# Output projection of a gated-delta-net block: feature halves of the first output units between the last chunk's steps

## The chip, the cores and the metric

The kernel runs on one core of one Trainium2 chip. The metric is the device time of one execution in microseconds; the kernel before took 1717.13 us in the median of three runs (1716.76 to 1719.14).

## What is computed

One block of a hybrid network over 16 meta tokens and 1024 tokens of 1024 features, all in fp32. A gated delta rule over chunks makes `o`; it is normalised per head, gated with `silu(z)`, and mixed with a causal pooling branch `y_b`. The mixed `y` goes through `w_out`, is added to the stream, and a convolved, gated MLP follows.

```python
def step(state, inp):
    q_i, k_i, u_i, w_i, qk_i, gt_i = inp
    v_new = u_i - jnp.einsum('bhck,bhkv->bhcv', w_i, state)
    o_i = jnp.einsum('bhck,bhkv->bhcv', q_i, state) + jnp.einsum('bhcs,bhsv->bhcv', qk_i, v_new)
    state = state * gt_i[..., None, None] + jnp.einsum('bhck,bhcv->bhkv', k_i, v_new)
    return state, o_i
...
o = (o * lax.rsqrt(jnp.mean(o * o, axis=-1, keepdims=True) + NORM_EPS)
     * head_norm.astype(jnp.float32) * jax.nn.silu(zf))
...
g_a, g_b = jnp.split(jax.nn.sigmoid(gate_pre), 2, axis=-1)
y = g_a * y_a + g_b * y_b
return jnp.einsum('bld,de->ble', y, w_out)
```

## The kernel before, in words

Every engine has one program written out by hand; the engines meet in counting semaphores only, and each queue works in the order in which the code stands. Features lie on the partitions, in eight tiles of 128 (`KT`), tokens along the free dimension.

**Products in three passes.** A large product takes an fp32 matrix apart into a high part (`u_hi`, `w_hi`) and what is left (`u_lo`, `w_lo`) and sums three matmuls for each of the eight feature tiles. A *unit* is one tile of 128 output features over one of three blocks of 342 tokens (`OBLOCKS`): 24 matmuls of 342 columns into one of three PSUM banks `gb`. Its weights are one tile of 512 KB: SyncE loads it to `w_raw`, ScalarE makes `w_hi` (`w_high`), GpSimd makes `w_lo` (`w_low`), three slots in turn. The semaphore `s_wlo` tells TensorE that a tile is ready.

**The chunks.** The delta rule runs over nine chunks of 128 tokens, all eight heads at once. A chunk has the steps P1 (keys times state), V (new values), O (outputs), SU (state) and OT (transposes of the output), besides those that invert a triangular matrix (X0 to Y2). In a chunk, matmul units of other projections stand between the steps to cover their latency; the last chunk's P1, V and O (L1153) have no units between them. After O, ScalarE copies the output from PSUM to `orx` and VectorE scales it with `output_scale`; `orx` is the buffer `vb`. `ot_d`, `za_d` and `yg_d` are DRAM tensors with each head's output, gated `z` and gated pooling branch. The last head's gates are still in `zs` and `gs`; `gated(8)` finishes `gs`, and ScalarE stores it to `yg_d`.

**The input of the output projection.** For each of the three token blocks `b`, SyncE's `load_y` brings `yo` from `ot_d`, `yz` from `za_d` and `yg` from `yg_d` (1.4 MB each) into one of two sets of buffers, block 2 into that of block 0. The second set lies where the chunk's buffers lay: `yo` of block 1 overlaps `vb`, so its load waits for OT. VectorE's `y_low` computes yo x yz + yg for the eight feature tiles in two halves of four; after each half ScalarE's `y_high` makes `u_hi` and VectorE subtracts to make `u_lo`, and counts `s_y`. `OUT_PLAN` gives the order of TensorE's work: units (0,0) and (1,0) (output tile, block), OT, then (2,0), (3,0), (4,0), (5,0), then (3,1), (4,1), (5,1), (3,2) and so on. Weight tiles 0 to 5 are used first, and tile `k` goes to the slot of `k - 3`. Tile 5 is loaded by SyncE behind block 1's `yz` and `yg` (L684), and ScalarE takes its high part after it evicts unit (2,0). Only the first unit of a block waits for `s_y`, once for each half.

## Time and profile before

| What | Time or count |
|---|---|
| Median of three runs | 1717.13 us (1716.76 to 1719.14) |
| Profiled execution, device time | 1718.44 us |
| Its span | 1716.6 us |
| TensorE, matmuls busy | 1675.1 us, 98% |
| VectorE busy | 896.9 us, 52% |
| ScalarE busy | 600.3 us, 35% |
| GpSimd busy | 494.5 us, 29% |
| Granted TensorE clock, mean | 0.994 of full speed |

Times in the timelines are microseconds from the start of the span. Busy time of a matmul is modelled and overlaps its neighbour, so TensorE's idle time before an instruction tells more than its busy share. The steps that the change touches lie between 830 and 890 us. PE is TensorE, DVE VectorE, ACT ScalarE, POOL GpSimd and SP SyncE; a q behind the name means the queue that issues DMAs.

### The profile page before, as it was taken

Reading aid. Unit: us, or ns where it says so; the run is one execution under the profiler, and the core shown is the slowest. Engines: PE = TensorE matmul, PEld = TensorE weight load, DVE = VectorE, ACT = ScalarE, POOL = GpSimd, SP = SyncE. Lnnn points to the kernel's source line nnn. Section 1 sums busy time; section 2 is a strip of 40 time slices with the busy share of each in tenths; the row PEclk is TensorE's granted clock in tenths of the full one; section 3 lists DMA queues with packets and bytes.
Section 4 is the critical chain, followed back from the end, with each engine's and each line's share of the span. In section 5 each row is a group of like instructions: output and inputs, shape, how many; then the busy total and the mean of one; then the engine's idle time right before and its main releaser. Section 6 shows DMA issues by size and latency. Waiting matters only on the chain.

```text
span 1716.6 us, 30495 instructions
## 1 busy us (share of the span) xinstructions
PE 1675.1 (98%) x12103; PEld 1603.8 (93%) x12103; DVE 896.9 (52%) x969; ACT 600.3 (35%) x982; POOL 494.5 (29%) x473
## 2 busy tenths in 40 slices
PE   7999999998999999999899999999999999999997
PEld 6999999998899999999899998998998998989986
DVE  5556454574444545444542665544545446455447
ACT  6333465544443434434333431221221211212214
POOL 3212212255445344453221132121212211221210
PEclk9999999999999999999999999999999999999999
DMA  5222443358555464554883121111111111211112
GB/s 182 71 93 97 131 147 90 92 157 142 149 167 140 119 158 114 141 163 109 208 270 97 38 62 50 37 49 49 49 37 39 59 49 37 61 48 38 49 37 98
DMA packets 242511, 168.23 MB, mean 98 GB/s; under 512 B 43913, under 2 KB 228840, under 8 KB 241306
## 3 DMA queue, kind: packets, MB, share of 16 engines
q1 hardware_dynamic: 209494, 135.30, 28.4%
q10 hardware_dynamic: 32740, 32.08, 5.6%
q8 instruction: 36, 0.59, 0.1%
q14 instruction: 17, 0.14, 0.0%
q0 software_dynamic: 224, 0.12, 0.0%
HBM read 125.10 MB, written 42.37 MB: 98 GB/s over the span
## 4 chain that ended last, share of the span: by engine, by line
PE 90%; DVE 3%; issue 2%; POOL 1%; POOLq 1%; ACT 1%; DMA 1%; DVEq 0%; ACTq 0%; SPq 0%
PE gb L878 66%; PE db L1224 11%; PE db L1022 4%; PE mb L1224 2%; PE db L936 1%; POOL w_lo L761 1%; PE db L1093 1%; PE db L1092 1%; DVE cacc L1735 1%; POOLq L810 1%; DMA yo<-ot_d 1%; POOLq L807 1%; DVE fino L2153 0%; PE db L1019 0%; PE db L1164 0%
## 5 line engine op out<-in xcount | busy, mean ns | idle before, releaser
L878 PE MATMUL gb<-u_hi,w_hi 128*128 128x342 f32 (+2 forms) x2520 | 821.9, 326 | 8.6 <-DVE u_lo L2021 5.1
L878 PE MATMUL gb<-u_lo,w_hi 128*128 128x342 f32 (+2 forms) x2520 | 809.5, 321 | 0.0
L878 PE MATMUL gb<-u_hi,w_lo 128*128 128x342 f32 (+2 forms) x2520 | 806.8, 320 | 0.0
L761 POOL TENSOR_TENSOR w_lo<-w_raw,w_hi 128x1024 fp32r<-128x1024 f32 x130 | 327.9, 2526 | 1048.8 <-ACT w_hi L1268 1048.7
L878 PEld LDWEIGHTS gb<-u_hi,w_hi 128*128 128x128 f32 x2520 | 477.4, 189 | 12.9 <-issue 9.2
L878 PEld LDWEIGHTS gb<-u_lo,w_hi 128*128 128x128 f32 x2520 | 477.6, 190 | 0.4
L878 PEld LDWEIGHTS gb<-u_hi,w_lo 128*128 128x128 f32 x2520 | 477.1, 189 | 0.0
L1268 ACT ACTIVATE w_hi<-w_raw 128x1024 fp32r<-128x1024 f32 x130 | 135.6, 1052 | 5.5 <-ACT tm L1367 5.2
L1735 DVE SCALAR_TENSOR_TENSOR cacc<-xb,prm,cacc 128x1040 f32<-128x1040 f32 x72 | 124.6, 1731 | 10.4 <-issue 8.4
L2118 DVE TENSOR_TENSOR h<-h,db 128x512 f32<-128x512 f32 x138 | 92.5, 684 | 42.2 <-PE db L1224 41.8
L1634 ACT ACTIVATE a_hi<-cv 128x1024 fp32r<-128x1024 f32 x21 | 22.3, 1060 | 248.8 <-PE db L1224 200.5
L1224 PE MATMUL db<-w_hi,a_hi 128*128 128x512 f32 x276 | 109.1, 395 | 0.1
L1224 PE MATMUL db<-w_lo,a_hi 128*128 128x512 f32 x276 | 109.1, 395 | 0.0
L1224 PE MATMUL db<-w_hi,a_lo 128*128 128x512 f32 x276 | 109.0, 395 | 0.0
L1619 ACT ACTIVATE xv<-gb 128x342 f32<-128x342 f32 x63 | 28.8, 458 | 188.1 <-PE gb L878 188.1
L2072 DVE TENSOR_SCALAR cg<-xg,prm 128x1024 f32<-128x1024 f32 x22 | 16.6, 754 | 138.9 <-ACT xg L1619 134.3
L1732 DVE TENSOR_SCALAR cacc<-xb,prm 128x1040 f32<-128x1040 f32 x24 | 18.3, 762 | 120.8 <-ACT xb L1389 96.6
L1389 ACT ACTIVATE xb<-gb 128x346 f32<-128x346 f32 (+1 forms) x63 | 28.8, 459 | 128.1 <-PE gb L878 128.0
L2074 DVE SCALAR_TENSOR_TENSOR cg<-xg,prm,cg 128x1024 f32<-128x1024 f32 x22 | 70.2, 3191 | 3.5 <-issue 3.4
L805 POOL TENSOR_TENSOR upd<-blk,sol 64x15 f32<-64x15 f32 (+4 forms) x135 | 48.4, 358 | 72.7 <-DMA blk<-blk_d 55.0
L1224 PEld LDWEIGHTS db<-w_hi,a_lo 128*128 128x128 f32 x276 | 51.7, 187 | 12.7
L1224 PEld LDWEIGHTS db<-w_hi,a_hi 128*128 128x128 f32 x276 | 51.8, 188 | 12.6 <-DVE a_lo L2142 0.5
(264 smaller groups left out, 1824.0 us busy)
## 6 DMA issues: line engine op xcount, KB each, us to landing
w_raw<-in_w_in SPq DMA_DIRECT2D x53, 512.0 KB, 4.2
w_raw<-in_w_up SPq DMA_DIRECT2D x44, 512.0 KB, 3.8
w_raw<-in_w_down SPq DMA_DIRECT2D x22, 512.0 KB, 3.5
qkT_d<-sl ACTq DMA_DIRECT2D x16, 576.0 KB, 2.8
kv_d<-tm ACTq DMA_DIRECT2D x16, 576.0 KB, 3.4
tk<-kv_d SPq DMA_DIRECT2D x9, 1024.0 KB, 7.6
w_raw<-in_w_out SPq DMA_DIRECT2D x11, 512.0 KB, 8.6
kT<-qkT_d SPq DMA_DIRECT2D x9, 512.0 KB, 5.0
```

The source lines that it names most:

```text
L761: pool.tensor_tensor(lo, w_raw[:, n % SLOTS, :], hi.bitcast(F32), ALU.subtract).then_inc(s_wlo, 1)
L805: pool.tensor_tensor(out, low[:, j, j + 1:].unsqueeze(2).broadcast_to([n, rest, j + 1]), inv[:, j, 0:j + 1].unsqueeze(1).broadcast_to([n, ...
L878: mm = pe.matmul(gb[:, bank, 0:w], wt, u, start=(k == 0 and m == 0), stop=(k == KT - 1 and m == 2))
L1022: return lambda o, m: pe.matmul(o, a[:, m, :], b[:, m, :], start=True, stop=True)
L1224: mm = pe.matmul(down_bank(u, n == W_LAST), a, wt, start=(q == 0 and m == 0), stop=(q == 1 and m == 2))
L1268: act.activation(wp_hi[:, :] if n == W_WPOOL else w_hi[:, n % SLOTS, :], w_raw[:, n % SLOTS, :], ACT.Copy).then_inc(s_whi, 1)
L1389: act.activation(xb[:, j % 3, 3 + o:3 + o + w], gb[:, b, 0:w], ACT.Copy).then_inc(s_gfree, 1)
L1619: act.activation(dst[:, o:o + w], gb[:, b, 0:w], ACT.Copy).then_inc(s_gfree, 1)
L1634: act.activation(a_hi[:, q, :], cv[:, :], ACT.Copy).then_inc(s_ahi, 1)
L1735: t = dve.scalar_tensor_tensor(cacc[:, :], xb[:, slot, j:j + T], tap(j), cacc[:, :], ALU.mult, ALU.add)
L2074: dve.scalar_tensor_tensor(dst[:, c0:c1], src[:, c0 + 1:c1 + 1], tap(1), dst[:, c0:c1], ALU.mult, ALU.add)
L2118: dve.tensor_tensor(dst, dst, down_bank(u, isinstance(i, int) and i == FFN_ITERS - 1), ALU.add).then_inc(s_dnfree, 1)
```

## The change

- **TensorE** runs the first feature halves of units (0,0), (1,0) and (2,0) early, the first between V and O, the others behind O. At their old place only the second halves stand. The first of them waits for the first half of block 0's input (`s_y` 1).
- **The last output** is copied to `kd` (the decayed keys, used last by the state update) instead of `vb`, so ScalarE waits for `s_kd` first.
- **SyncE** loads block 1's `yo` directly behind its `yz`, without the wait for OT.
- **VectorE** prepares `y` by halves. The product and sum of block 0's first half stand ahead of P1's subtraction and `gated(8)` behind it; for blocks 1 and 2 the steps of both halves are interleaved.
- **ScalarE** makes block 0's first `u_hi` half ahead of V's eviction, stores the last gates after V instead of at the end of the chunk, and takes block 1's `u_hi` before it evicts unit (4,0) instead of (5,0).

```diff
+        orx_last = kd
+        def output(c):
+            return orx_last if isinstance(c, int) and c == NCH - 1 else orx
...
             load_y(1, za_d, yz)
+            load_y(1, ot_from, yo)
             sp.wait_ge(s_yg, 16 * (HEADS + 1))
             load_y(1, yg_d, yg)
             load_out(5)
-            sp.wait_ge(s_ps["OT"], 2 * NCH)
-            load_y(1, ot_from, yo)
             sp.wait_ge(s_y, 2)
...
-            for name, prev in (("P1", TOP_X), ("V", LAST_Y), ("O", "P1")):
-                step(name, NCH - 1, (prev, 2 * (NCH - 2 if prev in LATER else NCH - 1)))
+            def first_half(n):
+                o, w = OBLOCKS[0]
+                w_ready(W_OUT + n)
+                pe.wait_ge(s_gfree, U_OUT - 3 + n + 1)
+                pe.wait_ge(s_y, 1)
+                unit(W_OUT + n, n, o, w, 0, KT // 2)
+            step("P1", NCH - 1, (TOP_X, 2 * (NCH - 2)))
+            step("V", NCH - 1, (LAST_Y, 2 * (NCH - 1)))
+            first_half(0)
+            step("O", NCH - 1, ("P1", 2 * (NCH - 2)))
+            first_half(1)
+            first_half(2)
...
-                    for hf in range(2):
+                    for hf in range(1 if q < 3 else 0, 2):
...
+            y_high(0, (0,))
             act_step("V", NCH - 1)
-            y_high(0)
+            gates_stored(HEADS - 1)
+            act.wait_ge(s_kd, NCH)
             act_step("O", NCH - 1)
+            y_high(0, (1,))
             act_step("SU", NCH - 1)
...
-                    if n == 5 and b < 2:
+                    if (n, b) in ((4, 0), (5, 1)):
                         y_high(b + 1)
...
+            def y_times(b, hf):
+                s = b % 2
+                dve.wait_ge(s_yin[s], 32 * (b // 2 + 1))
+                for ks, z in y_part(b, hf, zs, yz):
+                    dve.tensor_tensor(yo[s][:, ks, :], yo[s][:, ks, :], z, ALU.mult)
+            def y_plus(b, hf):
+                s = b % 2
+                dve.wait_ge(s_ygin[s], 16 * (b // 2 + 1))
+                drain()
+                for ks, g in y_part(b, hf, gs, yg):
+                    t = dve.tensor_tensor(yo[s][:, ks, :], yo[s][:, ks, :], g, ALU.add)
+                t.then_inc(s_y1, 1)
...
+            y_times(0, 0)
+            y_plus(0, 0)
             dve_step("P1", NCH - 1, True)
-            y_low(0)
+            y_low(0, 0)
+            gated(8, HEADS - 1)
+            drain()
+            y_times(0, 1)
+            y_plus(0, 1)
             output_sums(NCH - 1)
+            y_low(0, 1)
             output_scale(NCH - 1)
-            y_low(1)
-            y_low(2)
+            for b in (1, 2):
+                y_times(b, 0)
+                y_plus(b, 0)
+                y_times(b, 1)
+                y_low(b, 0)
+                y_plus(b, 1)
+                y_low(b, 1)
```

On SyncE's queue, behind the last load of block 0, before (`yz_102`, `yg_103`, `yo_104` are the buffers of block 1, those with 98 to 100 of blocks 0 and 2; `w_raw<-in_w_out` is a weight tile, the first one here tile 4 and the second tile 5):

```order
L658 DMA yg_100<-yg_d 128x7x342 [waits s_kd,s_vb,s_yg,s_ev_Y1,s_rd]
L508 DMA w_raw<-in_w_out 128x8x128 [waits s_wlo]
L658 DMA yz_102<-za_d 128x8x342 [waits s_za,s_ps_O]
L658 DMA yg_103<-yg_d 128x8x342 [waits s_yg]
L508 DMA w_raw<-in_w_out 128x8x128 [waits s_wlo]
L658 DMA yo_104<-ot_d 128x8x342 [waits s_ps_OT]
L658 DMA yz_98<-za_d 128x8x342 [waits s_y]
```

The same stretch of SyncE's queue now:

```order
L663 DMA yg_100<-yg_d 128x7x342 [waits s_kd,s_vb,s_yg,s_ev_Y1,s_rd]
L513 DMA w_raw<-in_w_out 128x8x128 [waits s_wlo]
L663 DMA yz_102<-za_d 128x8x342 [waits s_za,s_ps_O]
L663 DMA yo_104<-ot_d 128x8x342
L663 DMA yg_103<-yg_d 128x8x342 [waits s_yg]
L513 DMA w_raw<-in_w_out 128x8x128 [waits s_wlo]
L663 DMA yz_98<-za_d 128x8x342 [waits s_y]
```

Block 1's `yo` has moved from behind weight tile 5 to ahead of it, and ahead of `yg`.

On VectorE, from the eviction of the last Y2 step to the end of block 0's first half, before (`vb<-vb,db` is P1's subtraction, `gs<-gs,yl` is `gated(8)`):

```order
L1878 TENSOR_SCALAR rr<-db 64x2x64
L1975 TENSOR_TENSOR gs<-gs,yl 128x1026 [waits s_yl,s_gfree]
L1883 TENSOR_TENSOR vb<-vb,db 128x512 [waits s_ps_P1,s_vb]
L1883 TENSOR_TENSOR vb<-vb,db 128x512 [waits s_ps_P1]
L2012 TENSOR_TENSOR yo_99<-yo_99,yz_98 128x1368 [waits s_yin0]
L2012 TENSOR_TENSOR yo_99<-yo_99,yz_98 128x1026
L2012 TENSOR_TENSOR yo_99<-yo_99,zs 128x342
L2016 TENSOR_TENSOR yo_99<-yo_99,yg_100 128x1368 [waits s_ygin0]
```

The same place on VectorE now:

```order
L1902 TENSOR_SCALAR rr<-db 64x2x64
L2032 TENSOR_TENSOR yo_99<-yo_99,yz_98 128x1368 [waits s_yin0]
L2039 TENSOR_TENSOR yo_99<-yo_99,yg_100 128x1368 [waits s_ygin0]
L1907 TENSOR_TENSOR vb<-vb,db 128x512 [waits s_ps_P1,s_vb]
L1907 TENSOR_TENSOR vb<-vb,db 128x512 [waits s_ps_P1]
L2046 TENSOR_TENSOR u_lo<-yo_99,u_hi 128x4x342 [waits s_yhi]
L2000 TENSOR_TENSOR gs<-gs,yl 128x1026 [waits s_yl,s_gfree]
```

The product and the sum of block 0's first half have moved ahead of P1's subtraction; the `gs` product has moved behind it and behind the first `u_lo`.

## Rows read from the trace of the kernel before

**Rows 1.** The page, section 1: busy us, share of span, instructions of TensorE.
```profile
PE 1675.1 (98%) x12103; PEld 1603.8 (93%) x12103; DVE 896.9 (52%) x969; ACT 600.3 (35%) x982; POOL 494.5 (29%) x473
```

**Rows 2.** TensorE timeline, 835:890: start us, us, instruction, count, idle before and releaser.
```profile
838.24 2.02 PE L1022 MATMUL db<-vb,rr 128*128 128x128 f32 x16 [0.95 <-DVE vb L1883]
...
840.34 0.46 PE L1092 MATMUL db<-st,qdt 128*128 128x128 f32 x2
...
847.45 0.39 PE L878 MATMUL gb<-u_hi,w_hi 128*128 128x342 f32 x1 [3.30 <-DVE u_lo L2021]
...
874.50 0.40 PE L878 MATMUL gb<-u_hi,w_hi 128*128 128x342 f32 x1 [1.82 <-DVE u_lo L2021]
```

**Rows 3.** Chain that ended last, 780:920: start us, us, what.
```profile
847.45 9.30 PE gb L878 x48
```

**Rows 4.** ScalarE timeline, 800:900.
```profile
837.29 0.34 ACTq L1543 DMA_DIRECT2D yg_d<-gs  x1
...
844.28 1.34 ACT L1564 ACTIVATE u_hi<-yo 128x1368 fp32r<-128x1368 f32 x1 [3.38 <-DVE yo L2016]
...
865.19 0.46 ACT L1595 ACTIVATE ht<-gb 128x342 f32<-128x342 f32 x1 [1.98 <-PE gb L878]
...
868.95 0.46 ACT L1595 ACTIVATE ht<-gb 128x342 f32<-128x342 f32 x1 [3.30 <-PE gb L878]
...
880.07 0.46 ACT L1595 ACTIVATE ht<-gb 128x342 f32<-128x342 f32 x1 [5.50 <-PE gb L878]
```

**Rows 5.** Two-microsecond windows; the first row is the header.
```profile
core 0: us, PE busy (x) PEld busy (x) DVE busy (x) ACT busy (x) POOL busy (x), PEclk, DMA share, GB/s
...
850.00:852.00 2.00, 2.00 (x9) 2.00 (x8) 1.23 (x4) 0.73 (x2) 0.00 (x0) 0.52 1.07 231
...
868.00:870.00 2.00, 2.00 (x14) 2.00 (x13) 1.93 (x3) 0.46 (x1) 0.00 (x0) 1.00 1.07 391
...
876.00:878.00 2.00, 2.00 (x9) 2.00 (x8) 0.00 (x0) 0.00 (x0) 0.00 (x0) 0.50 1.11 336
```

**Rows 6.** VectorE timeline, 800:900.
```profile
832.77 1.21 DVE L1878 TENSOR_SCALAR rr<-db 64x128 f32<-64x128 f32 x4 [1.01 <-PE db L1076]
...
837.29 1.28 DVE L1883 TENSOR_TENSOR vb<-vb,db 128x512 f32<-128x512 f32 x2
...
838.50 3.67 DVE L2012 TENSOR_TENSOR yo<-yo,yz 128x1368 f32<-128x1368 f32 x2
```

**Rows 7.** Instructions on tile yo: count, ns min/median/max, starts, forms.
```profile
L2012 DVE TENSOR_TENSOR yo<-yo,yz x6: 1217/1580/2528, 838.5 to 880.3; 128x1368 f32<-128x1368 f32 x5, 128x1026 f32<-128x1026 f32 x1
```

**Rows 8.** GpSimd timeline, 800:900.
```profile
837.23 2.36 POOL L761 TENSOR_TENSOR w_lo<-w_raw,w_hi 128x1024 fp32r<-128x1024 f32 x1 [13.15 <-ACT w_hi L1268]
...
863.29 2.40 POOL L761 TENSOR_TENSOR w_lo<-w_raw,w_hi 128x1024 fp32r<-128x1024 f32 x1 [2.63 <-ACT w_hi L1268]
```

**Rows 9.** SyncE queue timeline, 780:920: start of the issue, its us.
```profile
829.03 0.37 SPq L658 DMA_DIRECT2D yg<-yg_d  x1
...
844.18 0.37 SPq L658 DMA_DIRECT2D yz<-za_d  x1
...
845.21 3.53 SPq L508 DMA_DIRECT2D w_raw<-in_w_out  x1
...
869.88 0.37 SPq L658 DMA_DIRECT2D yo<-ot_d  x1
```

**Rows 10.** DMA issues, 829:829.4: count, KB, us from issue to landing.
```profile
yg<-yg_d SPq DMA_DIRECT2D x1, 1197.0 KB, 8.1
```

**Rows 11.** DMA issues, 837:837.5.
```profile
yg_d<-gs ACTq DMA_DIRECT2D x1, 513.0 KB, 4.1
```

**Rows 12.** DMA issues, 844:844.5.
```profile
yz<-za_d SPq DMA_DIRECT2D x1, 1368.0 KB, 9.4
```

**Rows 13.** DMA issues, 845:846.
```profile
w_raw<-in_w_out SPq DMA_DIRECT2D x1, 512.0 KB, 16.9
```

**Rows 14.** DMA issues, 869:870.
```profile
yo<-ot_d SPq DMA_DIRECT2D x1, 1368.0 KB, 8.9
```

More of the change, by code:

```diff
@@ L1102, in step @@
                     pe.wait_ge(s_on, c + 1)
-                    each([], turned(orx))
+                    each([], turned(output(c)))
             def same_banks(name, among):
@@ L1184, in _ @@
                     w_ready(k)
-                    pe.wait_ge(s_gfree, U_OUT - 3 + q + 1)
-                    for hf in range(2):
+                    if q >= 3:
+                        pe.wait_ge(s_gfree, U_OUT - 3 + q + 1)
+                    for hf in range(1 if q < 3 else 0, 2):
                         if (n, b) in FIRST_OF_BLOCK:
@@ L1513, in act_step @@
                         act.activation(heads(ots, h), dbank(name, h), ACT.Square).then_inc(s_osq, 1)
-                        act.activation(heads(orx, h), dbank(name, h), ACT.Copy).then_inc(s_ev[name], 1)
+                        act.activation(heads(output(c), h), dbank(name, h), ACT.Copy).then_inc(s_ev[name], 1)
                 elif name == "SU":
@@ L1522, in act_step, with gates_stored, gates @@
                                   ots[:, :, :]).then_inc(s_ot, 16)
-            def gates(u, i):
+            def gates_stored(i):
+                act.wait_ge(s_gg, i + 1)
+                act.dma_start(yg_d[bass.ds(i * P, P), :], gs[:, :]).then_inc(s_yg, 16)
+            def gates(u, i, last):
                 t, b = divmod(u, 3)
@@ L1540, in gates @@
                     w_high(W_ZG + 3 + t, i)
-                if u == 8:
-                    act.wait_ge(s_gg, i + 1)
-                    act.dma_start(yg_d[bass.ds(i * P, P), :], gs[:, :]).then_inc(s_yg, 16)
+                if u == 8 and not last:
+                    gates_stored(i)
             def chunk(i, last):
@@ L1548, in chunk @@
                     for u in units_after(name):
-                        gates(u, i)
+                        gates(u, i, last)
                 act.wait_ge(s_ot, 16 * i + 16)
@@ L1556, in _, with y_high @@
             chunk(HEADS - 1, True)
-            def y_high(b):
+            def y_high(b, parts=(0, 1)):
                 o, w = OBLOCKS[b]
-                for hf in range(2):
+                for hf in parts:
                     ks = slice(4 * hf, 4 * hf + 4)
@@ L1915, in output_scale @@
                 dve.wait_ge(s_ev["O"], 2 * c + 2)
-                dve.tensor_tensor(orx[:, :, :], orx[:, :, :], per_head(orr), ALU.mult).then_inc(s_on, 1)
+                m = output(c)
+                dve.tensor_tensor(m[:, :, :], m[:, :, :], per_head(orr), ALU.mult).then_inc(s_on, 1)
             decays(0)
@@ L1988, in chunk, with y_part, y_low @@
                     for u in units_after(name):
-                        gated(u, i)
+                        if not (last and u == 8):
+                            gated(u, i)
+            def y_part(b, hf, kept, loaded):
+                o, w = OBLOCKS[b]
+                ks = FEATURE_HALVES[hf]
+                if b == 0 and hf == 1:
+                    yield slice(ks.start, KT - 1), loaded[0][:, ks.start:KT - 1, :]
+                    yield slice(KT - 1, KT), kept[:, o:o + w].unsqueeze(1)
+                else:
+                    yield ks, loaded[b % 2][:, ks, :]
+            def y_times(b, hf):
[10 more added lines that the diff above has]
+                t.then_inc(s_y1, 1)
+            def y_low(b, hf):
+                o, w = OBLOCKS[b]
+                ks = FEATURE_HALVES[hf]
+                dve.wait_ge(s_yhi, 2 * b + hf + 1)
+                dve.tensor_tensor(u_lo[:, ks, o:o + w], yo[b % 2][:, ks, :], u_hi[:, ks, o:o + w].bitcast(F32),
+                                  ALU.subtract).then_inc(s_y, 1)
             chunk(0, False)
```

24 lines of the change are left out of this document (removed).

## Prediction, made before the changed kernel was run

> **What bounds the kernel now.** I read the page first: TensorE is busy 98% of the span [rows 1], so only what it waits for, or what it does at the low clock, can be won or lost. The timeline of TensorE around the change [rows 2] shows three stands: 0.95 us before the last chunk's V product, 3.30 us between the O product and the first output unit, and 1.82 us before the first unit of token block 1. Both long ones end with VectorE's `u_lo`. After each of them the granted clock falls: it reads 0.52 in 850 to 852 and 0.50 in 876 to 878 (that is 1.2 GHz in place of 2.4), against 1.00 in 868 to 870 [rows 5]. A unit costs 3.76 us at the high clock (two evictions, 865.19 and 868.95) [rows 4]. The chain of waits has the first two units, 48 matmuls, at 9.30 us [rows 3], where 7.5 were due: 1.8 lost. The unit that starts at 874.50 [rows 2] is evicted at 880.07 [rows 4], 5.6 us later: 1.8 lost again. So the most that the change can win is about 3.3 + 1.8 + 1.8 + 1.8, with the 0.95, 9.7 us.
>
> **The front: halves before the first unit.** VectorE now multiplies and adds the first feature half of block 0 ahead of the P1 subtraction. It is free of the Y2 step at 832.77 + 1.21 = 834.0 [rows 6]; a 1368-wide pass takes 1.58 [rows 7], so the product ends at 835.6. The sum needs `yg`, issued at 829.03 [rows 9] and landing 8.1 us later [rows 10], at 837.1. It ends at 838.8 at the best. Only then come the two P1 subtractions, 1.28 us together, which started at 837.29 [rows 6]. V needs the first of them and starts at 838.8 + 0.7 = 839.5, 1.3 us later than at 838.24 [rows 2]. The final `gs` product, which stood there in the way, is moved behind them, and that saves nothing, since `yg` is later than it. V takes the 2.1 us to O's start at 840.34 [rows 2], so it ends at 841.6.
>
> Behind V stands the new first half of unit 0, which waits for the `u_lo` of this half: ScalarE's `u_hi` takes 1.34 [rows 4] from 838.8, and VectorE's subtraction 1.58 more (taken as the product's). GpSimd matters here. Its `w_lo` pass starts at 837.23 and takes 2.36 [rows 8]; the first product after it started at 838.50 [rows 6] and one of its kind took 2.53 us instead of 1.58 [rows 7], so it ended about 1.45 us behind GpSimd's end at 839.6. I read that as one waiting for the other. If VectorE's sum is ahead, GpSimd runs from 838.8 to 841.2, and the subtraction from 841.2 to 842.8. The half unit (1.9) then ends at 844.7 and O (3.8, from 840.34 to 847.45 - 3.30 = 844.15) [rows 2] at 848.5: O ends 4.3 us later than before. Two more half units bring TensorE to 852.3, and the second feature half is ready at 852.7: O's square and copy on ScalarE to 849.8, `u_hi` to 851.1, `u_lo` to 852.7. TensorE then stood 2.2, 1.2 and 0.4 us in pieces where it had stood 0.95 and 3.30. With two half units (3.8), the transposes of the last output (0.9), a half (1.9) and two units (7.5) it is ready for the sixth unit, (5,0), at 866.8. Before, that was 868.95, when unit (4,0) was evicted [rows 4]. So the front yields 2.1 us, mostly the low clock that I leave out here.
>
> The Trainium skill, SBUF — State Buffer, section SBUF: two separate sides, says that VectorE and GpSimd share a port pair under an exclusive lock, so that a VectorE instruction with two SBUF inputs and a GpSimd instruction never overlap, and the first to start makes the other wait. The trace agrees as far as that one 2.53 us pass goes. By that rule it counts which starts first at 837.2, and this is a rival below, priced there from the rows.
>
> **The loads of block 1.** `yo` no longer waits for the transposes, because the last output stands in `kd`, and it is issued beside `yz`, ahead of `yg` and of weight tile 5. All of them wait for the end of O, now 4.3 us later. `yg` also waits for the store of the last gates, about 4.1 us [rows 11] from 844.4 (behind `gated(8)`), so it is out at 848.5 and does not decide. What is queued behind matters: weight tile 5 was issued at 845.21 [rows 9] and landed 16.9 us later [rows 13], at 862.1. Its conversion was over at 863.29 + 2.40 = 865.7 [rows 8], 3.6 us after landing, and unit (5,0) took it at 868.95: 3.3 us to spare. Now this tile is 4.3 us later for O and has 1.4 MB more ahead of it in the same queue. At 391 GB/s, as in 868 to 870, this takes 3.6 us; at 231 GB/s, as in 850 to 852 [rows 5], 6.1. I take 4.0, since loads of `yo` ran in the faster stretches. That makes 862.1 + 4.3 + 4.0 = 870.4, and 874.0 with its conversion; another 0.5 for a `w_lo` pass that meets a VectorE product of block 1, 874.5. TensorE waits from 866.8 for 7.7 us where it had not waited at all.
>
> After a stand the unit takes 5.6 us, so unit (5,0) ends at 880.1. The stand of 1.82 before block 1 is gone, since that block's first half is ready near 876: `yg` lands ahead of tile 5, by 869.5, and a sum, a product and the `u_lo` are 4.7 us, up to 1.8 more where GpSimd's pass stands between them. Before, its first unit began at 874.50 and took 5.6, as if from 876.3 at the high clock. So the change comes out 880.1 - 876.3 = 3.8 us behind.
>
> Block 2 stays hidden: its `yo` was issued at 869.88 [rows 9] and landed after 8.9 [rows 14], 878.8. The queue held work all this while, so it moves by the same 4.3 to 883.1. Product, sum, product, `u_lo` are 6.3 us, to 889.4, against TensorE's need at 880.1 + 11.3 = 891.4. Without these 2 us of cover, a later `yo` would cost what exceeds them. The order in halves costs VectorE no more passes than before. ScalarE's earlier `y_high` calls hold up one eviction each, hidden by the three PSUM banks. All behind block 2 is paced by TensorE and moves with it.
>
> **The sum.** The profiled execution took 1718.44 us (1716.6 span and 1.8 around it), which gives 1722.2. It is 1.3 above the median of the runs, 1717.13; the same 3.8 on the median gives 1720.9, and that is my forecast.
>
> **Rivals.** (a) The three loads run faster than `yz` did, which took 9.4 us to land [rows 12]. With the rate of 868 to 870 for `yz` and `yg` each saves 6.1 - 3.6 = 2.5 us: tile 5 lands at 865.4, TensorE stands 2.2 us and block 1 starts at 872.8 at the high clock, 3.5 us ahead: 1713.6. With `yg` alone faster it is 2.5 better than the forecast, 1718.4. For it: the same kind of load ran at both rates. Against it: `yz` of block 1, which started on an idle queue, needed all of its 9.4 us. (b) The tile isn't late and the change does all that it can here: unit (5,0) starts at 866.8, block 1 at 870.6, 5.7 ahead of 876.3: 1711.4, faster. It needs tile 5 landed by 866.8 - 3.6 = 863.2, within 1.1 us of where it landed before although O ends 4.3 later; it decides for the change from about 865 on. (c) GpSimd's `w_lo` starts first, at 837.23, and VectorE's sum waits to 839.6: V starts at 842.0, the half unit at 844.1, 1.3 us later than above, TensorE stands 4.7 us ahead of V and the clock falls there as it did after 3.30, for 1.8 more. All loads move along: 3.8 + 1.3 + 1.8 = 6.9, 1724.0. For it: `yg` lands at 837.1 and the pass began at 837.23, a tenth apart.
>
> **The numbers.** A measurement of this kernel can tell about 0.2%, 3.4 us, from no change. The forecast's own case has 0.45: its 1719 to 1722.5 comes from 3.6 to 6.1 us for the added load and from a low clock at the front; 0.27 of it is slower, 0.18 within. (a) has 0.30, of which 0.10 faster and 0.20 within. (b) has 0.10, faster; (c) 0.15, slower. Together 0.20 faster, 0.38 within, 0.42 slower. The range of 8 in 10 leaves out (b) and the far end of (c): 1712.5 to 1724.
>
> **What would show it.** Right: TensorE stands several us ahead of the sixth output unit, released by GpSimd's `w_lo`, whose `w_hi` waits for tile 5's landing at about 870; O ends near 848.5; V waits about 2 us; no stand before block 1. Wrong: tile 5 lands by 864, or the queue serves it ahead of `yg`; `yg` of block 0 lands well before 837; or a new stand before block 2 greater than 1 us.

## The result, and the profile after

The changed kernel took 1723.84 us in the median of 17 runs, the kernel before 1716.17 us in the median of 17 runs on the same chip. The ratio is 1.0044 (1.0036 to 1.0053): 7.5 us slower. The forecast was 1720.9 us, within 1712.5 to 1724.0, with "slower" as the likeliest of the three. One execution of f1_front_back, below, took 4985.75 us and is left out of its ratio; what held it up is not known. The profiled execution took 1725.94 us, its span 1724.1.

The page, section 1, of the kernel after. TensorE is busy 3.4 us longer than in [rows 1], with the same 12103 matmuls; the mean granted clock of the profiled execution is 0.991 where it was 0.994.

```profile
PE 1678.5 (97%) x12103; PEld 1607.2 (93%) x12103; DVE 899.3 (52%) x969; ACT 600.2 (35%) x982; POOL 494.8 (29%) x473
```

The last Y2 eviction starts at 830.01 here and started at 832.77 before [rows 6]. So times below are also given from that instruction on, as "+x". The 2.8 us come from far ahead of the change (last section).

TensorE after, timeline, the rows with a stand (in brackets the idle time ahead of it and what ended it):

```profile
839.22 3.75 PE L1026 MATMUL db<-vb,rr 128*128 128x128 f32 x16 [4.69 <-DVE vb L1907]
853.51 0.39 PE L882 MATMUL gb<-u_hi,w_hi 128*128 128x342 f32 x1 [0.37 <-DVE u_lo L2046]
873.44 0.65 PE L882 MATMUL gb<-u_hi,w_hi 128*128 128x342 f32 x1 [5.67 <-POOL w_lo L765]
895.63 0.42 PE L882 MATMUL gb<-u_hi,w_hi 128*128 128x342 f32 x1 [2.42 <-DVE u_lo L2046]
```

Against [rows 2] the 3.30 and the 1.82 are gone, the 0.95 before V has become 4.69, and two are new: 5.67 us ahead of unit (5,0) and 2.42 us in the middle of unit (3,2), ahead of its second feature half. Together 13.2 us stand where 6.1 stood.

VectorE after, timeline. V's wait is explained by the second and third rows; the last two are the `u_lo` of block 2's two halves:

```profile
831.14 1.57 DVE L2032 TENSOR_TENSOR yo<-yo,yz 128x1368 f32<-128x1368 f32 x1
834.62 3.62 DVE L2039 TENSOR_TENSOR yo<-yo,yg 128x1368 f32<-128x1368 f32 x1 [1.91 <-DMA yg<-yg_d]
838.27 1.28 DVE L1907 TENSOR_TENSOR vb<-vb,db 128x512 f32<-128x512 f32 x2
...
889.31 1.58 DVE L2046 TENSOR_TENSOR u_lo<-yo,u_hi 128x1368 fp32r<-128x1368 f32 x1 [2.95 <-ACT u_hi L1585]
...
893.99 1.58 DVE L2046 TENSOR_TENSOR u_lo<-yo,u_hi 128x1368 fp32r<-128x1368 f32 x1 [1.41 <-ACT u_hi L1585]
```

GpSimd after, timeline, the pass of the third weight tile (before: [rows 8], first row) and that of tile 5:

```profile
834.46 2.34 POOL L765 TENSOR_TENSOR w_lo<-w_raw,w_hi 128x1024 fp32r<-128x1024 f32 x1 [13.23 <-ACT w_hi L1286]
...
871.03 2.35 POOL L765 TENSOR_TENSOR w_lo<-w_raw,w_hi 128x1024 fp32r<-128x1024 f32 x1 [9.09 <-ACT w_hi L1286]
```

GpSimd began at 834.46, VectorE's sum at 834.62, and the sum took 3.62 us where its kind takes 1.58: it ended 1.4 us behind GpSimd's end at 836.80. The subtraction for P1, and V with it, stood behind it.

SyncE's queue after, timeline (before: [rows 9]):

```profile
849.41 0.37 SPq L663 DMA_DIRECT2D yz<-za_d  x1
849.83 0.58 SPq L663 DMA_DIRECT2D yo<-ot_d  x1
850.45 3.38 SPq L663 DMA_DIRECT2D yg<-yg_d  x1
853.88 5.19 SPq L513 DMA_DIRECT2D w_raw<-in_w_out  x1
```

ScalarE after, timeline: the high part of tile 5, then the eviction of unit (4,1) and the first `u_hi` of block 2:

```profile
869.90 1.06 ACT L1286 ACTIVATE w_hi<-w_raw 128x1024 fp32r<-128x1024 f32 x1 [9.06 <-DMA w_raw<-in_w_out]
...
887.59 0.46 ACT L1619 ACTIVATE ht<-gb 128x342 f32<-128x342 f32 x1 [3.31 <-PE gb L882]
887.94 1.34 ACT L1585 ACTIVATE u_hi<-yo 128x1368 fp32r<-128x1368 f32 x1
```

Block 1's first load is issued at +19.40, right behind O's end, for which it waits; before it was at 844.18, +11.41 [rows 9]. Tile 5 is landed at 869.90, +39.9, and was at 862.16, +29.4.

The windows of TensorE's clock after (columns as in [rows 5]) show that V runs at the low level (1.2 GHz, 0.50) behind its stand, and so do the unit behind the 5.67 and the half behind the 2.42:

```profile
840.00:842.00 2.00, 2.00 (x11) 2.00 (x11) 2.00 (x2) 0.60 (x1) 0.00 (x0) 0.50 0.00 0
842.00:844.00 2.00, 2.00 (x10) 2.00 (x10) 1.91 (x3) 0.60 (x1) 0.00 (x0) 0.50 0.08 31
...
876.00:878.00 2.00, 2.00 (x9) 2.00 (x8) 0.58 (x2) 1.47 (x2) 0.00 (x0) 0.50 1.07 367
...
896.00:898.00 2.00, 2.00 (x10) 2.00 (x9) 0.00 (x0) 0.00 (x0) 0.00 (x0) 0.54 0.68 207
```

The account from the last Y2 eviction on: O ends 8.0 us late; unit (3,1) is evicted 6.5 us late (883.82 against 880.07 [rows 4], each less its Y2 time); the first weight pass behind the loads (`w_lo` of tile 6) is 10.5 late, and the end of the span 10.3. That is the 7.5 by which the two spans differ and the 2.8 by which the profile of after was ahead at the last Y2 eviction. Each is one execution; for the change the ratio counts.

### The profile page after: what moved, and what is told of

It reads as the page before. It is cut to its first block, busy times and chain, and to the rows that moved or that the text cites. A ratio compares the mean times of both kernels' runs of the same rounds, so it can differ in the third digit from the quotient of the medians.

```text
span 1724.1 us, 30501 instructions
## 1 busy us (share of the span) xinstructions
PE 1678.5 (97%) x12103; PEld 1607.2 (93%) x12103; DVE 899.3 (52%) x969; ACT 600.2 (35%) x982; POOL 494.8 (29%) x473
## 4 chain that ended last, share of the span: by engine, by line
PE 89%; DVE 3%; issue 2%; DMA 2%; POOL 1%; POOLq 1%; ACT 1%; DVEq 0%; SPq 0%; ACTq 0%
PE gb L882 65%; PE db L1242 11%; PE db L1026 4%; PE mb L1242 2%; PE db L940 1%; POOL w_lo L765 1%; PE db L1097 1%; DMA w_raw<-in_w_out 1%; PE db L1096 1%; DVE cacc L1759 1%; DVE fino L2194 1%; POOLq L814 1%; POOLq L811 1%; DMA yg<-yg_d 0%; PE db L1181 0%
## 5 line engine op out<-in xcount | busy, mean ns | idle before, releaser
L1242 PEld LDWEIGHTS db<-w_hi,a_lo 128*128 128x128 f32 x276 | 51.8, 188 | 12.6
L1242 PEld LDWEIGHTS db<-w_hi,a_hi 128*128 128x128 f32 x276 | 51.8, 188 | 12.6 <-DVE a_lo L2183 0.5
```

The lines of the kernel that those rows point to most:

```text
L1242: mm = pe.matmul(down_bank(u, n == W_LAST), a, wt, start=(q == 0 and m == 0), stop=(q == 1 and m == 2))
```

## The experiments

Every kernel was timed against the kernel before on the same chip. The ratios are those of the runs. The last three columns are from each kernel's profile, in us from the last Y2 eviction: O's end (issue of block 1's `yz`), the start of tile 6's `w_lo`, and the end of the span. Those are single samples of a time that varies by some us, and the ratios decide. Beside the e runs the kernel before took 1714.80 us in the median, beside the f runs 1715.74 and beside the g runs 1719.46. A ratio is not the quotient of two medians and can differ from it, by 0.12 points at most (g2).

| Kernel | Ratio (95%) | O's end | tile 6 | end |
|---|---|---|---|---|
| before | 1 | 11.4 | 60.0 | 883.8 |
| after | 1.0044 (1.0036 to 1.0053) | 19.4 | 70.5 | 894.1 |
| e1_tile5_early | 1.0022 (1.0012 to 1.0031) | 18.2 | 64.4 | 887.6 |
| e2_wlow_later | 1.0033 (1.0022 to 1.0044) | 18.8 | 70.3 | 893.8 |
| e3_high2_sooner | 1.0025 (1.0016 to 1.0034) | 19.5 | 66.7 | 890.0 |
| e4_yo1_late | 1.0063 (1.0047 to 1.0079) | 18.1 | 69.8 | 893.9 |
| f1_front_back | 1.0025 (1.0014 to 1.0035) | 10.6 | 63.8 | 887.2 |
| f2_front_tile5_high2 | 1.0007 (0.9998 to 1.0016) | 10.6 | 60.4 | 883.7 |
| f3_loads_only | 0.9987 (0.9978 to 0.9995) | 11.4 | 57.8 | 881.7 |
| f4_loads_tile5 | 0.9984 (0.9974 to 0.9995) | 11.4 | 56.5 | 880.3 |
| g1_best | 0.9987 (0.9978 to 0.9996) | 11.5 | 58.7 | 882.6 |
| g2_pe_only | 1.0030 (1.0015 to 1.0044) | 16.3 | 67.9 | 891.5 |
| g3_p1_first | 1.0057 (1.0043 to 1.0071) | 19.9 | 70.7 | 894.0 |

**e1: the changed kernel with tile 5 loaded right behind tile 4, ahead of block 1's loads.**

```diff
             load_out(4)
+            load_out(5)
...
             load_y(1, za_d, yz)
             load_y(1, ot_from, yo)
...
             load_y(1, yg_d, yg)
-            load_out(5)
```

> The changed kernel, with the load of weight tile 5 issued directly behind tile 4, ahead of block 1's three loads. Theory 1 (the queue): tile 5 lands near 845 instead of 869.9, TensorE no longer stands 5.7 us ahead of unit (5,0) and has no low clock behind it, and the program is 4 to 7 us shorter, so 0.5 to 3.5 us above the kernel before; part may come back as a wait before block 1 for yg, which lands near 866. Theory 2 (the front): the loss is made before O by V's wait of 4.7 us with its low clock; block 1's inputs then hold TensorE up where tile 5 did, and the time stays within 1.5 us of the changed kernel, 6 to 8 us above the kernel before.

1719.13 us: 0.22 points better than the changed kernel. TensorE's waits of e1 (total, times, longest):

```profile
PE gb L882 <- DVE u_lo L2046: 5.5, 4, 2.5
PE db L1026 <- DVE vb L1907: 4.7, 1, 4.7
PE gb L882 <- POOL w_lo L765: 0.2, 1, 0.2
```

One of the four waits for `u_lo` is new, in the middle of block 1's first unit, timeline:

```profile
875.45 0.42 PE L882 MATMUL gb<-u_hi,w_hi 128*128 128x342 f32 x1 [2.46 <-DVE u_lo L2046]
```

The wait of 5.67 is gone, and 2.7 us of waits for block 1 came in its place (0.28 and 2.46). So the late weight tile is a cause, as forecast, and it is about half of the loss: 0.22 points are 3.8 us, a little less than the 4 to 7 expected.

**e2: the changed kernel with the high part of the third weight tile (tile 2) taken behind V's evictions**, so that GpSimd can't start beside the first sum.

```diff
-                if b == 2:
+                if b == 2 and not (last and u == 8):
                     w_high(W_ZG + 3 + t, i)
...
             act_step("V", NCH - 1)
+            w_high(W_OUT + 2)
             gates_stored(HEADS - 1)
```

> The changed kernel, with ScalarE's high part of weight tile 2 moved from the end of the last chunk to behind V's evictions, so that GpSimd's low part of it can't run beside VectorE's sum of block 0's first half. Theory 1 (GpSimd and VectorE exclude each other): the sum takes 1.6 us instead of 3.6, V waits about 2.3 us instead of 4.7, the end of O and all loads behind it come 2 to 4 us sooner (more if the clock stays high), and the program is 2 to 4 us shorter than the changed kernel, 3.5 to 5.5 above the kernel before. Theory 2 (the sum was slow for another reason, as the landing of yg): the sum still takes over 3 us and nothing changes.

1720.7 us. VectorE of e2, and GpSimd's pass where it is now:

```profile
834.38 1.58 DVE L2040 TENSOR_TENSOR yo<-yo,yg 128x1368 f32<-128x1368 f32 x1 [3.29 <-DMA yg<-yg_d]
...
843.14 2.68 DVE L2040 TENSOR_TENSOR yo<-yo,gs 128x342 f32<-128x342 f32 x1
```

```profile
842.41 3.03 POOL L765 TENSOR_TENSOR w_lo<-w_raw,w_hi 128x1024 fp32r<-128x1024 f32 x1 [23.11 <-ACT w_hi L1286]
```

The same sum with nothing beside it takes 1.58 again, and a pass that took 0.51 now takes 2.68 because GpSimd starts ahead of it. The exclusion is shown in both places. What V gained was small (its wait went from 4.69 to 4.0), since `yg` took 9.7 us to land in this profile instead of 8.3; 2.3 us of wait were expected. The ratio's interval overlaps that of the changed kernel: what this one collision costs isn't told apart from nothing by the runs.

**e3: the changed kernel with block 2's `u_hi` one unit sooner.**

```diff
-                    if (n, b) in ((4, 0), (5, 1)):
-                        y_high(b + 1)
+                    if (n, b) == (4, 0):
+                        y_high(1)
+                    elif (n, b) == (4, 1):
+                        y_high(2, (0,))
+                    elif (n, b) == (5, 1):
+                        y_high(2, (1,))
```

> The changed kernel, with ScalarE's high parts of block 2 taken one half ahead of the eviction of unit (4,1) and one ahead of that of (5,1), instead of both ahead of (5,1). Theory 1: the wait of 2.4 us in the middle of unit (3,2) comes from the first high part standing behind the eviction of (4,1), while its input was ready 3 us before; the wait is gone and the program 2 to 2.5 us shorter, about 5 above the kernel before. Theory 2: the landing of block 2's yo sets it; the wait stays and the time is that of the changed kernel.

1719.67 us, 0.19 points better than the changed kernel. TensorE's waits of e3:

```profile
PE gb L882 <- POOL w_lo L765: 5.8, 2, 5.6
PE db L1026 <- DVE vb L1911: 4.7, 1, 4.7
PE gb L882 <- DVE u_lo L2050: 0.4, 1, 0.4
```

The stand in unit (3,2) is gone and the two others are as they were. ScalarE in the changed kernel had this half's sum from 884.9 on (883.28 + 1.58), but held `u_hi` behind the eviction of unit (4,1) at 887.59, 3.1 us later. That is the step which I had costed at nothing. Its price is 3.3 us by the ratios and 4.1 by the profiles, more than its 2.42, which fits the low clock behind the stand.

**e4: the changed kernel with block 1's `yo` back behind tile 5 and OT.** It keeps the halves and undoes the loads.

```diff
             load_y(1, za_d, yz)
-            load_y(1, ot_from, yo)
             sp.wait_ge(s_yg, 16 * (HEADS + 1))
             load_y(1, yg_d, yg)
             load_out(5)
+            sp.wait_ge(s_ps["OT"], 2 * NCH)
+            load_y(1, ot_from, yo)
             sp.wait_ge(s_y, 2)
```

> The changed kernel, with block 1's yo loaded behind weight tile 5 and behind the transposes again, as before; all else as changed. Theory 1 (yo ahead of tile 5 costs): tile 5 lands 4 to 5 us earlier, near 865, the wait ahead of unit (5,0) falls to 1 or 2 us, but a wait before block 1 for yo takes up most of it: the program is 0 to 2 us shorter than the changed kernel. Theory 2 (loading block 1 together is right and only its place hurts): the time is longer than the changed kernel's by 1 us or more, since yo lands last and block 1 is late.

1726.63 us. Waits of e4:

```profile
PE gb L883 <- DVE u_lo L2047: 6.9, 4, 2.5
PE db L1027 <- DVE vb L1908: 4.7, 1, 4.7
PE gb L883 <- POOL w_lo L766: 3.6, 2, 3.3
```

TensorE's wait for tile 5 is 2.3 us shorter without `yo` ahead of it, but it waits for block 1 again (1.69 and 2.46 of the 6.9). The ratio is 0.19 points above that of the changed kernel; the two intervals still overlap a little (1.0047 against 1.0053), so that this load helps even here is likely and not proved. That it harms, as my sum had it with its 4.0 us for the added load, is not what the runs say.

**f1: the front put back.** The changed kernel with O directly behind V and all three halves behind O, and with P1's subtraction ahead of block 0's product and sum.

```diff
-            first_half(0)
             step("O", NCH - 1, ("P1", 2 * (NCH - 2)))
+            first_half(0)
             first_half(1)
...
-            y_times(0, 0)
-            y_plus(0, 0)
             dve_step("P1", NCH - 1, True)
+            y_times(0, 0)
+            y_plus(0, 0)
...
-            y_high(0, (0,))
             act_step("V", NCH - 1)
+            y_high(0, (0,))
```

> The changed kernel with the order of its front undone: VectorE subtracts P1 ahead of block 0's product and sum, ScalarE evicts V ahead of the high part, and TensorE runs O directly behind V, the first halves of the three units behind O. Loads and the rest as changed. Theory 1 (what delays O delays all three loads of block 1, tile 5 and block 2): O ends some 8 us sooner than in the changed kernel, counted from the output store of the chunk before, the wait ahead of unit (5,0) falls from 5.7 to about 1 us, the 2.4 us in unit (3,2) stay, and the time is 1.5 us below the kernel before (ratio 0.999, between 0.997 and 1.001). Theory 2 (the loads are too slow whatever O does): tile 5 still comes over 3 us late and the ratio stays above 1.002.

1718.93 us against 1715.74. O ends 8.8 us sooner than in the changed kernel, but only some 3 us of it reach the end. TensorE's stands in f1:

```profile
842.49 0.39 PE L882 MATMUL gb<-u_hi,w_hi 128*128 128x342 f32 x1 [2.46 <-DVE u_lo L2046]
850.31 0.39 PE L882 MATMUL gb<-u_hi,w_hi 128*128 128x342 f32 x1 [1.94 <-DVE u_lo L2046]
868.40 0.65 PE L882 MATMUL gb<-u_hi,w_hi 128*128 128x342 f32 x1 [2.30 <-POOL w_lo L765]
```

A fourth, of 2.42 us, stands in unit (3,2). The expectation was missed. V doesn't wait any more and O ends at +10.6, but the first half starts at +13.05, only 1.6 us sooner than the first unit did before (847.45 is +14.68, [rows 2]): its product met GpSimd's pass and took 3.08 us. The second half is 1.9 us late, because VectorE makes `gs` and that half's product and sum only behind the first `u_lo`. So the halves break one stand into two.

Why tile 5 is still late is seen on SyncE's queue, timeline, and in its waits:

```profile
840.47 0.58 SPq L663 DMA_DIRECT2D yo<-ot_d  x1
853.11 0.37 SPq L663 DMA_DIRECT2D yg<-yg_d  x1
```

```profile
SPq L663 <- DMA yg_d<-gs: 12.0, 1, 12.0
```

The queue stood 12.0 us between `yo` and `yg` until the store of the last gates had landed, and tile 5 stands behind `yg`. The change had moved `gated(8)` behind the first `u_lo`, so ScalarE issues that store at 843.51, +14.07 (before: 837.29, +4.52, [rows 4]). It then runs beside the loads of `yz` and `yo` and takes 9.6 us, where it took 4.1 [rows 11]. In the changed kernel the same late store did no harm, because O was later still. Tile 5's high part starts at +35.1 in f1 and at +31.4 in f3, where the store is in its old place and O ends 0.8 us later. So f1 puts the front back but not the store, and isn't a clean trial of an undelayed O.

**f2: f1 with tile 5 early (e1) and block 2's `u_hi` sooner (e3).**

```diff
             load_out(4)
+            load_out(5)
...
             load_y(1, yg_d, yg)
-            load_out(5)
...
+                    elif (n, b) == (4, 1):
+                        y_high(2, (0,))
```

> As the run with the front undone, with tile 5 loaded behind tile 4 and block 2's high parts taken a unit sooner. Theory 1: no wait ahead of unit (5,0), none or under 1 us in block 2; 4 to 5 us below the kernel before, ratio 0.997. Theory 2 (the landing of block 2's yo bounds what is left): TensorE waits 2 us or more for block 2, and the ratio is 0.998 to 1.000.

1716.21 us, ratio 1.0007: even with the kernel before, short of what was expected. Its waits:

```profile
PE gb L882 <- DVE u_lo L2050: 7.2, 4, 2.5
PE gb L882 <- POOL w_lo L765: 0.2, 1, 0.2
```

Four stands of `u_lo` are left, 7.2 us together, where there were two before, 3.30 and 1.82 [rows 2]. Two are in the front (2.47 and 1.95) and two in the middle of the first units of blocks 1 and 2 (0.45 and 2.35). Early loads and early `u_hi` are a gain of 0.18 points on f1. What takes away all that the loads bring (f4, below) is the front, the halves of blocks 1 and 2 and the late store together: `yg` of block 1 is held up here too and issued at +23.2, 12.6 us behind O's end.

**f3: the kernel before with only the last output in `kd` and block 1's `yo` beside its `yz`.**

```diff
+        orx_last = kd
...
             load_y(1, za_d, yz)
+            load_y(1, ot_from, yo)
             sp.wait_ge(s_yg, 16 * (HEADS + 1))
             load_y(1, yg_d, yg)
             load_out(5)
-            sp.wait_ge(s_ps["OT"], 2 * NCH)
-            load_y(1, ot_from, yo)
...
-                        act.activation(heads(orx, h), dbank(name, h), ACT.Copy).then_inc(s_ev[name], 1)
+                        act.activation(heads(output(c), h), dbank(name, h), ACT.Copy).then_inc(s_ev[name], 1)
...
+            act.wait_ge(s_kd, NCH)
             act_step("O", NCH - 1)
```

> The kernel before with one part of the change alone: the last output in kd, and block 1's yo loaded directly behind its yz, ahead of yg and tile 5. Theory 1 (with O in its old place tile 5 has slack for one load more): tile 5 lands 20.5 us after the first of the loads, near 864.7, its parts are ready at 868.3, in time for unit (5,0) at 868.9; the wait of 1.8 us before block 1 goes with its low clock, and the time is 2 to 3.5 us below the kernel before, ratio 0.998 to 0.9985. Theory 2 (the load order alone costs): TensorE waits 1 us or more for tile 5 and the ratio is 1.000 or more.

1713.55 us, ratio 0.9987: the loads alone make the kernel faster by 2.2 us, as expected. ScalarE of f3, where tile 5 lands:

```profile
860.08 1.06 ACT L1271 ACTIVATE w_hi<-w_raw 128x1024 fp32r<-128x1024 f32 x1 [2.23 <-DMA w_raw<-in_w_out]
```

This is 19.9 us behind the issue of the first of the four loads (840.13), 20.5 in the changed kernel (849.41 to 869.90). The queue needs nearly the same time in both; only O's end has moved. The stand before block 1 is gone, and one of 1.07 before block 2 is new (881.02).

**f4: f3 with tile 5 right behind tile 4.**

```diff
             load_out(4)
+            load_out(5)
...
             load_y(1, yg_d, yg)
-            load_out(5)
```

> As the run with the loads alone, with tile 5 loaded behind tile 4. Theory 1: tile 5 had no wait left to remove, but block 1 and 2 land 1 to 2 us sooner: ratio 0.997 to 0.998. Theory 2: block 2's readiness is set by its VectorE and ScalarE steps, and the ratio is that of the loads alone.

1711.96 us, ratio 0.9984, the lowest of all and 0.6% below the changed kernel; the intervals of f3 and g1 overlap it nearly whole, so it is not told apart from them. Its waits:

```profile
PE gb L881 <- DVE u_lo L2026: 3.3, 1, 3.3
PE gb L881 <- issue: 1.6, 1, 1.6
PE db L1025 <- DVE vb L1887: 0.9, 1, 0.9
PE gb L881 <- POOL w_lo L764: 0.2, 1, 0.2
```

The stands before blocks 1 and 2 are gone, that of 3.30 behind O is left. The 1.6 lies behind this stretch.

**g1: an attempt at the whole.** f2, with block 0's first product in front of `gated(8)` at its old place, then P1's subtraction, then the sum, the second product and the first `u_lo`; the last gates are stored where they were before the change.

```diff
-                        if not (last and u == 8):
-                            gated(u, i)
+                        if last and u == 8:
+                            y_times(0, 0)
+                        gated(u, i)
...
-            y_times(0, 0)
+            dve_step("P1", NCH - 1, True)
             y_plus(0, 0)
-            dve_step("P1", NCH - 1, True)
+            y_times(0, 1)
             y_low(0, 0)
-            gated(8, HEADS - 1)
-            drain()
-            y_times(0, 1)
             y_plus(0, 1)
```

> A version meant to keep what helped. Loads as changed, but tile 5 behind tile 4; TensorE runs O directly behind V and the three first halves behind O; VectorE does block 0's first product ahead of the gs product (while it is idle), the gs product and P1's subtraction in their old place, then the sum; ScalarE evicts V first, stores the last gates as before, and takes block 2's high parts a unit sooner. Theory 1 (V and O undelayed, halves only fill the stand behind O): V waits 0.95 us, the stands behind O are under 1 us together, up to 3 us remain ahead of block 1, and the first matmul of block 2 comes about 49.5 us after VectorE's last Y2 eviction, against 54.5 before: 4 to 6 us below the kernel before, ratio 0.997. Theory 2 (whatever TensorE saves behind O it waits for again ahead of block 1, whose loads start at O's end): no better than the loads with tile 5 ahead, ratio 0.9984 or more.

1717.91 us against 1719.46, ratio 0.9987: no better than f4, though the stand of 3.30 behind O is gone. Its waits:

```profile
PE gb L882 <- DVE u_lo L2050: 5.5, 3, 2.5
PE db L1026 <- DVE vb L1910: 1.0, 1, 1.0
```

P1's subtraction is on time, V waits 1.0, O ends at +11.5. VectorE of g1 shows what is late instead:

```profile
858.97 2.62 DVE L2036 TENSOR_TENSOR yo<-yo,yz 128x1368 f32<-128x1368 f32 x1 [6.51 <-DMA yo<-ot_d]
863.84 1.58 DVE L2043 TENSOR_TENSOR yo<-yo,yg 128x1368 f32<-128x1368 f32 x1 [2.25 <-DMA yg<-yg_d]
...
878.02 1.58 DVE L2036 TENSOR_TENSOR yo<-yo,yz 128x1368 f32<-128x1368 f32 x1 [4.92 <-DMA yo<-ot_d]
```

TensorE, which wins 3 us behind O, is at blocks 1 and 2 sooner, and stands there: 1.55 us ahead of block 2 (884.41), whose `yo` landed at 878.0, and 1.53 and 2.45 us ahead of the second halves of the first units of blocks 1 and 2 (873.16 and 888.99). The first is a wait for the loads. The other two, 4.0 of the 5.5, come from the order of the halves on VectorE (next section, block 2). Against f2, g1 is 0.20 points better, the intervals just clear of each other (0.9996 and 0.9998); it has the gates' store in its old place (+4.52) and the new order in the front, and no run parts the two.

**g2: the changed kernel with only TensorE's order changed**, the half of unit (0,0) behind O instead of between V and O.

```diff
-            first_half(0)
             step("O", NCH - 1, ("P1", 2 * (NCH - 2)))
+            first_half(0)
             first_half(1)
```

> The changed kernel with one edit on TensorE: the first half unit stands behind O instead of between V and O. Theory 1 (the two delays of O add up: V's late start and the half unit): V still waits 4.7 us, O ends about 2.9 us sooner, so do all loads, and the ratio falls from 1.0044 to about 1.003. Theory 2 (only V's wait matters, the half unit fills a gap that would be there): O ends less than 1 us sooner and the ratio stays at 1.004.

Ratio 1.0030, V still waits 4.69 us, O ends 3.1 us sooner than in the changed kernel, and tile 5's wait falls from 5.7 to 4.9. O's end is as expected. The time isn't told apart from the changed kernel's: the intervals overlap (1.0044 against 1.0036), and the two medians of this round, 1726.61 and 1719.46, give 1.0042.

**g3: the changed kernel with P1's subtraction ahead of the sum** and V's eviction ahead of `u_hi`, the half still between V and O.

```diff
             y_times(0, 0)
-            y_plus(0, 0)
             dve_step("P1", NCH - 1, True)
+            y_plus(0, 0)
...
-            y_high(0, (0,))
             act_step("V", NCH - 1)
+            y_high(0, (0,))
```

> The changed kernel with P1's subtraction ahead of block 0's sum on VectorE, and V's evictions ahead of the high part on ScalarE; the half unit stays between V and O. Theory 1 (the half unit ties O to the first u_lo, and V's late start only shows where the wait is seen): V waits under 1 us, but TensorE stands 4 to 5 us ahead of the half unit, O ends within 1 us of where it did, and the ratio stays at 1.004 to 1.005. Theory 2 (V's late start is the cost): O ends 3 us or more sooner and the ratio is 1.0025 or less.

Ratio 1.0057, no better than the changed kernel. The two stands of g3 that matter:

```profile
841.69 2.02 PE L1026 MATMUL db<-vb,rr 128*128 128x128 f32 x16 [0.16 <-issue]
...
848.39 0.63 PE L882 MATMUL gb<-u_hi,w_hi 128*128 128x342 f32 x1 [4.68 <-DVE u_lo L2046]
```

V no longer waits, and the wait stands whole before the half unit instead, with O behind it: O ends at +19.9. So it is the half unit that ties O to the first `u_lo`. Freeing only V (g3) or only O (g2) gives 0 and 3.1 us; both (f1) give 8.8.

## Why the prediction came out as it did

**The direction and the main mechanism: right.** O is late, the loads of block 1 and tile 5 start at its end, tile 5 is last of four in its queue, and TensorE stands ahead of unit (5,0) until GpSimd's `w_lo`. e1 shows the last step, g2, g3 and f1 the first, f3 the middle one by contrast: the same four loads in the same order do no harm when O is in time. One sign of being wrong came true all the same, a new stand of over 1 us at block 2.

**The front: the forecast's own case failed, rival (c) happened.** I had let VectorE's sum start ahead of GpSimd and V start at 839.5; (c) had V at 842.0. V started at 839.22, +9.2, and 832.77 + 9.2 is 842.0. `yg` took 8.27 us instead of 8.1 and so landed 0.07 us behind the start of GpSimd's pass. The tenth did not decide it: in e1 `yg` took 8.13 and landed 0.04 ahead of GpSimd's start (834.71), the sum started at 834.75, and it waited all the same. The Trainium skill, SBUF — State Buffer, section SBUF: two separate sides, has the port pair under an exclusive lock that makes the later instruction wait; the trace agrees, 3.62 us against 1.58 in e2. V's wait is 4.7 in e1, e3, e4 and g2 too. (c) had O 7.4 us late, and 8.0 were measured. The 0.6 is the low clock: I had taken 1.8 us for every stand, from the two before, but behind the 4.69 V and the half unit took 6.43 us (839.22 to 845.65) where 2.1 + 1.9 were due, 2.4 lost.

**The load's term: a little too dear.** From O's end to tile 5's landing I had 21.9 us (848.5 to 870.4); it took 20.5, and the stand was 5.67, not 7.7. The other 0.6 is the conversion: 3.5 us from landing to unit (5,0) (869.90 to 873.44) where I had 4.1. TensorE came 3.7 us later than forecast, but so did O and the loads with it.

**Block 1: right.** There is no stand ahead of unit (3,1). It was evicted 6.5 us late; the forecast's 3.8, with 3.7 more for O and 1.4 and 0.6 less for the load and the conversion, is 5.5. The last 1.0 is the low clock again: unit (5,0) took 6.6 us behind its stand (873.44 to its eviction at 880.04), not 5.6.

**Block 2: wrong.** "Block 2 stays hidden", with 2 us of cover, was the step that failed. I counted `yo`'s landing at 883.1, product, sum, product, `u_lo` one behind the other, and left out that ScalarE takes `u_hi` only at its place in its queue, behind the eviction of unit (4,1). On the changed kernel's own clock `yo` was there at 881.6 and the sum at 884.9, and `u_hi` began at 887.94. The cover was counted to the first need, too, while the second half is needed half a unit later and is made 4.7 us later (889.31 to 893.99). The 2.42 us and the low clock behind it are the 3.3 us by which e3 is faster. "The order in halves costs VectorE no more passes" is true, but it makes the second half late. Before, both `u_lo` passes ran back to back; now the second starts 4.7 us behind the first, and half a unit takes 1.9. Stands of 2.35 to 2.46 us ahead of a block's second half are seen in the changed kernel, e1, e2, e4, f1, f2, g1 and g2, and none in the kernel before, f3 and f4, which have the old order. From block 2's first product to the start of the second half it is 9.8 us in f3 (873.13 to 882.97) and 11.0 in g1 (878.02 to 888.99); the first half starts 1.5 us sooner in g1 (6.4 against 7.9). No run puts back this order alone.

**The size.** 3.8 forecast, 7.5 measured, twice as much. On the profiles the terms above lead to the 6.5 at unit (3,1), and block 2 adds 4.0; e3 puts block 2 at 3.3 by the ratios. That makes some 10 us where the ratio has 7.5. The ratio's interval is 1.5 us either way and the profiles are single executions, so up to 2.5 us stay unexplained. That 1723.84 us is inside the range is luck: it is 2.9 us above the forecast and 0.2 below the upper end, and the kernel before had come down from 1717.13 to 1716.17 meanwhile.

**What the change is made of.** The loads alone are a gain of 2.2 us (f3). The halves on the old loads are a loss of some 11 (e4, 1.0063). The halves were to fill a stand of 3.30 us. Where the change put them they hold up both V and O, since the data for them (`yg`) comes only 4.5 us behind the last Y2 eviction, when P1's subtraction is due. g1 shows that this isn't forced: with the first product ahead of `gs` and the sum behind P1's subtraction V and O are on time and the 3.30 is gone. But its ratio, 0.9987, is that of the loads alone; the 3 us are lost again at blocks 1 and 2, in good part by the order of their halves.

**Open.** Whether the collision with GpSimd alone costs a measurable amount wasn't settled by e2. Why `yg` of block 0 takes 8.1 to 10.0 us for one load was not tried. And two parts of the change were never undone alone: the late store of the last gates, and the halves of blocks 1 and 2. A kernel like g1 with the old order there is the next to try.

## What to carry to other kernels

- Work put between two steps of a serial chain ties the chain's later step to that work's inputs. Ask what starts at the chain's end: here three loads of 1.4 MB and a weight tile. Once their cover is used up, a delay at the chain's end reaches TensorE.
- A stand that is worth 3 us may be cheaper than splitting it: f1 and f2 turned one of 3.30 into two, 2.47 and 1.95 in f2, at no gain seen. Work cut into halves pays only if the second half is ready when the first is used up; here it came 4.7 us later for 1.9 us of work.
- A late store that stands ahead of a load in some queue can be hidden by a worse delay, and show only when that one is mended (the 12.0 us of f1).
- When data are moved earlier or later, look for the instruction that hands them on in each queue. An engine with 65% idle time (ScalarE) still cost 3 us by an eviction that stood ahead of its `u_hi`.

## What the runs showed of the hardware

- **VectorE and GpSimd.** A VectorE pass over two SBUF tiles that starts after a GpSimd pass waits for it (3.62 and 3.08 us for 1.58, 2.68 for 0.51), each time ending about one normal pass behind GpSimd (1.4 us for the two of 1.58, 0.4 for the one of 0.51). Where VectorE is first, GpSimd waits (3.03 for 2.35 in e2). P1's subtraction, with one operand in PSUM, seems freer: in f1 both took 1.51 us together beside GpSimd's pass at 833.90 (1.28 elsewhere).
- **The low clock behind a stand.** It cost 1.8 us behind 3.30 and 1.82, 2.4 behind 4.69 and 2.8 behind 5.67 (unit (5,0) 6.60 us for 3.76). Not every stand of this size had it: the 2.46 us in e1 at 875.45 was followed by 0.50 in 877 to 879, but behind the 2.46 at 890.95 in the same run, and behind 2.46 in f1 at 842.49, the granted clock read 1.00.
- **The rate of the loads.** In the changed kernel the DMA engines moved 199 to 229 GB/s from 852 to 858 and 380 to 391 from 858 to 862. In f3 it was 186 and 191 in 844 to 848 and 376 in 848 to 850, and again 232 and 266 in 854 to 858. It is the same kind of load (1.4 MB in rows of 1368 bytes) each time. A slow stretch comes first in both, but it is not the only one. Its cause is open.
- **A store beside loads.** The store of the last gates (513 KB) took 4.1 us before and 4.2 in the changed kernel, ahead of the loads of block 1, and 9.6 in f1 and 9.1 in f2, beside them.
- **A part that isn't changed varies.** Between the stores of the first two chunks' outputs lie 56.95 us in the profile of before, 55.88 in after and 52.58 in e4, though these steps are the same. With the 1.84 us by which the first of these stores is earlier in after, the 1.07 make up the 2.8 us by which it is ahead at the last Y2 eviction. Over all the runs it is 52.58 (e4) to 59.76 (g3), and all three g runs have over 58.8; the kernel before was slower in that round too (1719.46 us against 1715.74 in the f round). Variation of this size fits the spread of single runs (1712.76 to 1719.14 us for the kernel before). The rows for before:

```profile
442.34 0.38 ACTq L1521 DMA_DIRECT2D ot_d<-ots  x1
499.29 0.41 ACTq L1521 DMA_DIRECT2D ot_d<-ots  x1
```
